# Reordering the head of an eight-core decoder-layer kernel: part of the first query projection ahead of the last adaLN chunk

## What is computed

```
ada = silu(c) @ w_ada + b_ada                 # shift, scale, gate
h = rms_norm(x, norm_g) * (1 + scale) + shift
z = h @ w_in                                  # 8704 columns: q, k, v of three groups, gates, branch B, merges
q = rope(rms_norm(z_q)); k = rope(rms_norm(z_k))     # per group and head
attn = softmax-weighted sum of three dilated causal window attentions
y_a = attn * silu(gate_a); y_b = u * spatial(layer_norm(v_b)) * silu(gate_b)
out = x + gate * ((sig(m_a) * (y_a @ w_branch_a) + sig(m_b) * (y_b @ w_branch_b)) @ w_out)
```

## Time and profile before

| | |
|---|---|
| median of 6 runs | 753.49 us (753.33 to 754.24) |
| the profiled execution's own time | 754.04 us |
| its span on the slowest core (core 7) | 752.5 us |
| spans of the eight cores | 748.7 to 752.5 us |
| PE busy on core 7 | 714.4 us, 95% of the span |
| DVE, ACT, POOL busy | 63%, 48%, 38% |
| DMA, mean over the span | 93 GB/s |

### The profile page before, as it was taken

One profiled execution on the slowest core, in us unless ns is written; L12 is line 12 of the kernel. 1 busy time (PEld: TensorE's weight loads), 2 busy tenths in 40 slices (PEclk: granted clock), 3 DMA queues, 4 the chain that ended last, 5 costly groups with the idle time before them and its releaser, 6 DMA issues.

```text
span 752.5 us, 14671 instructions; the slowest of 8 cores (748.7 to 752.5 us)
## 1 busy us (share of the span) xinstructions
PE 714.4 (95%) x4702; PEld 359.3 (48%) x4702; DVE 471.7 (63%) x788; ACT 361.1 (48%) x687; POOL 289.3 (38%) x370
## 2 busy tenths in 40 slices
PE   7778999999999999999999999999999999999994
PEld 2444455556655554445554444444444444444442
DVE  6437799986587778888788864466664233222333
ACT  3636888878645554556676645565221111111110
POOL 1405243342444455433434002577232343343343
PEclk9879999999999999999999999999999999999998
DMA  8994125034456657531111607139980223111324
GB/s 240 322 181 132 55 85 127 3 51 78 59 84 81 93 75 76 85 58 29 29 29 30 113 1 112 29 49 177 187 233 28 84 86 108 61 56 57 113 58 167
DMA packets 61243, 70.00 MB, mean 93 GB/s; under 512 B 39792, under 2 KB 46064, under 8 KB 60528
## 3 DMA queue, kind: packets, MB, share of 16 engines
q0 software_dynamic: 16352, 22.29, 21.0%
q1 hardware_dynamic: 42368, 38.39, 20.6%
q10 hardware_dynamic: 2448, 8.39, 2.8%
HBM read 74.82 MB, written 8.39 MB: 111 GB/s over the span
## 4 chain that ended last, share of the span: by engine, by line
PE 65%; DVE 9%; DMA 7%; issue 6%; ACT 6%; SPq 3%; POOL 2%; DVEq 0%; ACTq 0%; POOLq 0%
PE ps L249 57%; DVE arena L258 9%; ACT arena L258 6%; DMA arena<-w_ada 3%; SPq L261 3%; PE ps L651 2%; DMA arena<-arena 2%; DMA arena<-w_in 2%; POOL arena L258 2%; PE ps L544 2%; PE ps L687 2%; PE ps L692 1%; PE ps L609 1%; SPq L600 0%; PE ps L1048 0%
## 5 line engine op out<-in xcount | busy, mean ns | idle before, releaser
L249 PE MATMUL ps<-arena 128*128 128x512 bf16 x2596 | 582.5, 380 | 10.0 <-DVE arena L258 7.1
L249 PEld LDWEIGHTS ps<-arena 128*128 128x128 bf16 x2596 | 269.0, 107 | 291.9 <-issue 31.1
L258 POOL TENSOR_TENSOR arena<-arena 128x128 bf16<-128x128 f32 (+5 forms) x308 | 255.5, 838 | 395.3 <-DVE arena L258 332.1
L258 ACT ACTIVATE arena<-ps 128x1024 bf16<-128x1024 f32 (+2 forms) x283 | 192.1, 709 | 263.0 <-PE ps L249 137.1
L258 DVE TENSOR_TENSOR arena<-ps,arena 128x512 bf16<-128x512 f32 (+2 forms) x214 | 166.2, 798 | 58.8 <-PE ps L249 24.4
L258 ACT ACTIVATE arena<-arena 128x8 f32<-128x8 f32 (+7 forms) x264 | 108.9, 423 | 73.3 <-DVE arena L258 49.1
L258 DVE SCALAR_TENSOR_TENSOR arena<-arena,ps 128x512 f32<-128x512 f32 x80 | 54.3, 686 | 110.1 <-PE ps L249 92.1
L258 DVE TENSOR_TENSOR arena<-arena 128x1024 bf16<-128x1024 bf16 (+5 forms) x111 | 78.0, 705 | 23.1 <-POOL arena L258 10.7
L258 DVE TENSOR_REDUCE arena<-arena 128x8 f32<-128x512 bf16 x96 | 65.4, 685 | 42.7 <-ACT arena L258 42.2
L258 DVE SCALAR_TENSOR_TENSOR arena<-arena 128x512 f32<-128x512 f32 (+3 forms) x40 | 33.3, 831 | 11.8 <-DMA arena<-w_ada 4.3
L258 DVE TENSOR_SCALAR arena<-arena 128x512 bf16<-128x512 bf16 (+5 forms) x57 | 27.6, 484 | 11.4 <-DMA arena<-w_ada 7.6
(11 more groups left out here) (42 smaller groups left out, 186.7 us busy)
## 6 DMA issues: line engine op xcount, KB each, us to landing
arena<-x SPq DMA_DIRECT2D x32, 512.0 KB, 5.3
arena<-w_in POOLq DMA_DIRECT2D x9, 1024.0 KB, 14.2
arena<-w_in POOLq DMA_DIRECT2D x32, 256.0 KB, 5.6
arena<-w_ada SPq DMA_DIRECT2D x15, 512.0 KB, 15.0
out<-arena ACTq DMA_DIRECT2D x15, 512.0 KB, 5.6
arena<-w_adag SPq DMA_DIRECT2D x8, 512.0 KB, 7.8
arena<-w_out POOLq DMA_DIRECT2D x2, 1024.0 KB, 23.8
arena<-w_ba POOLq DMA_DIRECT2D x1, 1024.0 KB, 12.9
```

The costliest lines, as they stand in the source:

```text
L249: ins = e.matmul(out_ap, l, r, start=(i == 0), stop=(i == n - 1))
L258: P.op(eng, lambda e: getattr(e, meth)(*a, **kw), reads=reads, writes=writes)
```

## The change

Loads: x tile 3 is loaded ahead of adaLN chunk 2 instead of behind it. The first three q quarters are gated on the landing of x tile 2, the fourth on the second piece of chunk 3 (`wada3_2`), and the k and v quarters follow it in POOL's list. x tile 4 is gated on the fourth q quarter instead of the third.

Order: the tiles 1, 2 and 3 are normalised and transposed ahead of adaLN chunk 2, their scaling moves from ACT to DVE. `phase(0, 0)` and `phase(0, 1)` of the tiles 0, 1 and 2 come ahead of `ada_mm(2)`, their `phase(0, 2)` ahead of `ada_mm(3)`; tile 3 does its three quarters after `ada_ab(3)`. The spins are 8, then 12, then 16 behind the landing of `wada3_4`, instead of 8 and 14.

```diff
-            for t in ((0,), (1, 2), (3,), ())[c]:
+            for t in ((0,), (1, 2, 3), (), ())[c]:
                 x_load(t)
...
         sq_own(1)
-        x_prep(1)
+        rs_own(1)
         spin(4, 7)
         ada_mm(1)
-        ada_sum(2, 0, 3)
         ada_ab(1)
+        sc_own(1)
         x_transp(1, 4)
-        sq_own(2)
-        x_prep(2)
-        x_transp(2, 5)
-        for kc in range(4):
-            x_mods(kc, "act", 0, 2)
-        ada_sum(2, 3, 8)
+        for t in (2, 3):
+            sq_own(t)
+            rs_own(t)
+            sc_own(t)
+            x_transp(t, 3 + t)
+        for t in (0, 2):
+            for kc in range(4):
+                x_mods(kc, "act", t, 2)
+        for p_ in range(3):
+            load_w(0, 0, p_, p_ + 1, ["xs2"])
+        load_w(0, 0, 3, 4, ["wada3_2"])
+        for j in (1, 2):
+            for p_ in range(4):
+                load_w(j, 512 * j, p_, p_ + 1)
+        for t in range(4):
+            x_load(t + 4, gate=[("ws0p3", "ws1p2", "ws2p1", "ws2p3")[t]])
+        ada_sum(2)
         spin(8, 7)
-        ada_mm(2)
-        sq_own(3)
-        x_prep(3)
-        x_transp(3, 6)
-        ada_sum(3, 0, 4)
-        ada_ab(2)
...
-        for j in (0, 1, 2):
-            for p_ in range(4):
-                load_w(j, 512 * j, p_, p_ + 1, ["wada2_6"])
-        for t in range(4):
-            x_load(t + 4, gate=[("ws0p2", "ws1p2", "ws2p1", "ws2p3")[t]])
-        ada_sum(3, 4, 8)
-        spin(14, 7)
-        ada_col(3)
-        for kc in (6, 7):
-            x_mods(kc, "act", 0, 2)
-            x_mods(kc, "dve", 2, 2)
...
+        phase(0, 0, range(3))
+        phase(0, 1, range(3))
+        ada_mm(2)
+        ada_ab(2)
+        for t in (0, 2):
+            for kc in (4, 5):
+                x_mods(kc, "act", t, 2)
+        ada_sum(3)
+        phase(0, 2, range(3))
+        spin(12, 2)
+        spin(16, 2, ["wada3_4"])
+        ada_mm(3)
+        ada_ab(3)
+        for kc in (6, 7):
+            x_mods(kc, "act", 0, 2)
+            x_mods(kc, "dve", 2, 2)
         for j in range(3):
-            phase(0, j)
+            phase(0, j, (3,))
         last(0)
```

More of the change, by code:

```diff
@@ L472, in build_nc @@
         sq_own(1)
-        x_prep(1)
+        rs_own(1)
         spin(4, 7)
         ada_mm(1)
-        ada_sum(2, 0, 3)
         ada_ab(1)
+        sc_own(1)
         x_transp(1, 4)
-        sq_own(2)
-        x_prep(2)
-        x_transp(2, 5)
-        for kc in range(4):
-            x_mods(kc, "act", 0, 2)
-        ada_sum(2, 3, 8)
-        spin(8, 7)
-        ada_mm(2)
-        sq_own(3)
-        x_prep(3)
-        x_transp(3, 6)
-        ada_sum(3, 0, 4)
-        ada_ab(2)
-        for kc in (4, 5):
-            x_mods(kc, "act", 0, 2)
-        for kc in range(6):
-            x_mods(kc, "act", 2, 2)
-        for j in (0, 1, 2):
-            for p_ in range(4):
-                load_w(j, 512 * j, p_, p_ + 1, ["wada2_6"])
-        for t in range(4):
-            x_load(t + 4, gate=[("ws0p2", "ws1p2", "ws2p1", "ws2p3")[t]])
-        ada_sum(3, 4, 8)
-        spin(14, 7)
-        ada_col(3)
-        for kc in (6, 7):
-            x_mods(kc, "act", 0, 2)
-            x_mods(kc, "dve", 2, 2)
+        for t in (2, 3):
[15 more added lines that the diff above has]
+        ada_sum(2)
+        spin(8, 7)
         X("dve", "tensor_copy", ["misc"], ["gcol"], out=gcol, in_=gqk)
```

## The result

The changed kernel takes 759.11 us (median; 757.58 to 761.41) where the kernel before, run beside it, took 753.38 (752.68 to 755.13): a ratio of 1.0074, with a 95% interval of 1.0065 to 1.0082. It is slower by 5.6 us (0.0074 x 753.38); 753.7 with a range to 756.5 was forecast. The profiled execution took 759.17 us at a span of 757.6, on core 4.

What follows compares the result with a forecast made beforehand. TensorE was taken to bound the body (PE 95% busy), leaving only the head to gain. Tile 4's -0.8 plus the clock's +1.0 gave +0.2 us on 753.49: 753.7 us, range 751.0 to 756.5.

Steps and rivals of the forecast that it cites:

- The adaLN chunk: Last adaLN weight load: `wada3_2` at 41.9, whole chunk landing at about 45 us, as before (44.5).
- The fourth q quarter: Weight load gated on `wada3_2`: issued 0.6 us after it, 4.8 us long, landing at 47.3, at latest 50.8.
- the quiet window: Lightly loaded DMA stretch in the earlier profile: 4.8 us for a weight quarter, against 8.3 under load.
- its late bound: Latest landing allowed for x tile 4: 60.5 us, from a quarter at 50.8 plus 9.7.
- the term of x tile 4, the -0.8 us: ACT's start on tile 4, gated on the fourth q quarter: about 57.0 instead of 57.79, 0.8 us gained.
- The gain of 0.8 us from an earlier x tile 4: Same tile 4 claim: ACT starts about 57.0 instead of 57.79, whatever PE has saved.
- PE's own way: PE's path to the first q result of `last(0)`: about 53 (52 to 56) instead of 55.2, gaining 2 us.
- The clock: TensorE's granted clock behind PE's wait before tile 4's transpose: 1.0 us lost, bounds nothing to 2.9.
- the slow rival: PE's wait before tile 4's transpose lowers the clock: 2.9 us, 756.4 with tile 4 at its old time; chance 0.33.
- the case of x tile 4 at its late bound together with the low clock: Tile 4 landing at 60.5 and reduced TensorE clock behind its transpose; left outside the range, no total given.

Runs made afterwards that it cites:

- e3: Changed kernel with x tile 4 not gated at all: 755.96 us, ratio 1.0007 to the kernel before.
- e6: Changed kernel, x tile 4 ungated, chunk 2's columns before q, two chunk 3 sums before `ada_ab(2)`, 16 spins of 28: 753.45 us, ratio 0.9974.
- e1: Changed kernel with x tile 4 gated on the third q quarter again instead of the fourth: 756.44 us, ratio 1.0009 to the kernel before.
- e4: Kernel before with only x tile 4's gate moved, from the third q quarter to the second k quarter: 764.46 us, ratio 1.0097.
- e2: Changed kernel with 40 unused matmuls added on PE ahead of x tile 4's transpose: 759.78 us, ratio 1.006 to the kernel before.
- e8: Kernel before with x tile 4 not gated, nothing else changed: 755.56 us, ratio 0.9995.
- e5: Changed kernel with x tile 4 ungated and the 28 spins ahead of the last adaLN columns left out: 757.30 us, ratio 1.0023.

## Why the prediction was wrong

**The adaLN chunk: right.** `wada3_2` was forecast at 41.9 and landed at 40.0 to 43.0 on the eight cores; the chunk was forecast at about 45 and landed at 43.3 to 45.5.

**The fourth q quarter: the first term mis-sized.** The prediction took the quiet window's 4.8 us, to 47.3, and the loaded 8.3 as its bound. On the latest core of the changed kernel, 4, and on an early one, 1, the DMA views have these issues (queue, count, size, us from issue to landing):

```profile
arena<-w_in POOLq DMA_DIRECT2D x1, 256.0 KB, 6.8
arena<-x SPq DMA_DIRECT2D x1, 512.0 KB, 10.4
...
arena<-w_in POOLq DMA_DIRECT2D x1, 256.0 KB, 4.1
```

It took 6.8 us on core 4, 4.0 to 7.1 on the eight, and landed at 45.5 to 50.3. 50.8 had been the bound, and core 4 came about half a microsecond short of it. Part of the spread is a later start: on cores 1, 2, 5 and 6 the first of its packets move 1.2 us behind the issue, on cores 0, 3, 4 and 7 2.3 to 2.5 us behind it.

**x tile 4: its late bound, on the cores that count.** The chain is the one that the prediction drew, but its term was too small on the late cores. It took 10.4 us on core 4, where 9.7 was taken, and landed at 60.9, with 57.0 forecast and 60.5 as the bound. The 3.9 us between are 1.1 of the gate (42.97 for 41.9), 2.0 of the quarter (6.8 for 4.8), 0.7 of the tile and 0.1 of issue. On core 7, from which every term was taken, the forecast held in this execution: quarter at 47.7, tile at 57.0, first q result at 53.4, transpose at 60.03 where "within 1 us of 60.96" was written. **The step that failed is the term of x tile 4, the -0.8 us: it was made for core 7**, the slowest before, and its late bound was left to the edge of the range. On the core that ended last it measured +2.9 at the transpose. The time is that of the slowest of eight cores. With landings of the same transfer spread from 54.1 to 60.9, the latest one decides, and that lay at the bound.

**The gain of 0.8 us from an earlier x tile 4** did not come: on core 4, ACT began on it at 60.96 and not at about 57.0. Core 7's earlier transpose, 60.03 for 60.96, agrees with the forecast's 0.8 us, but it is not the core that ends last.

**PE's own way: right in the middle, worth nothing at the end.** 52 to 56 was forecast for the first q result, and it came at 51.3 to 55.5. But before, it was 52.0 to 55.2: the latest cores gained nothing, where 2 us had been expected. What was not seen is that `ada_sum(3)` stands behind `ada_ab(2)` on DVE, and that one behind PE's matmuls of quarter 1. DVE's timeline of core 4:

```profile
44.64 0.16 DVE L258 TENSOR_TENSOR arena<-ps,arena 128x4 f32<-128x4 f32 x1 [5.55 <-PE ps L408]
...
45.60 5.88 DVE L258 SCALAR_TENSOR_TENSOR arena<-arena 128x512 f32<-128x512 f32 x7
```

The prediction priced two sums of chunk 2 at 0.75 each and none of chunk 3's behind the wait. By e3 against e6 (ratios 1.0007 and 0.9974) undoing this order, together with 12 spins fewer, is worth 2.5 us.

**The clock: the slow rival's mechanism, at nearly its price.** The rival named the place (the transpose of x tile 4), the point ("x tile 4 after 57.5") and 2.9 us; it had a chance of 0.33. It happened where the prediction said, and cost 2.2 us of the span, against the 1.0 taken for the sum. The forecast's -0.8 + 1.0 became 2.9 + 2.2. The Trainium skill (TensorE: Matmul & The Clock Gate, Part 1, The HAM clock gate) has the throttled clock as the default state that activity releases; the trace agrees in direction, as 0.18 us of work in 2.8 was followed by 0.50, and 1.11 or 1.94 us of waiting was not.

**What was left out of the range.** The rival kept tile 4 "at its old time" and so came to 756.4; the case of x tile 4 at its late bound together with the low clock was left out by name. They are not independent: the same late tile moves the transpose and makes the wait that lowers the clock. By the prediction's own terms that case gives 753.49 + 2.7 (60.5 for 57.79) + 2.9 = 759.1, and by the measured ones 753.49 + 2.9 + 2.2 = 758.6; the changed kernel took 759.11. That the first agrees to the digit is luck, since its two terms are off by 0.2 and 0.7 us in opposite directions.

**Shown and open.** That x tile 4's gate is the cause is shown from both sides: e1 and e3 take it away and the loss goes, e4 adds it alone to the kernel before and a loss comes. That the clock has a part is shown by the cores of one execution (14.2 against 16.5 us to the next transpose) and by core 4 of e2, where the filled wait left it at 1.00. e8 shows that the gain of e6 is not the tile's; how much of that gain is the order of the sums and how much the fewer spins is open. Open, too, is why POOL's queue began 1.2 us after the issue on four cores and 2.3 to 2.5 us after it on the others.

## What to carry to other kernels

A new gate makes a chain of transfers: add their late landings, not their typical ones, and do so for the slowest core, since it sets the time. A late input in front of a dense TensorE stretch is paid twice, by the delay and by the clock behind it, so the two go into one case. Before moving work on one engine, look in the other engines' lists for what stands behind a wait on it: here, sums on DVE stood behind columns on PE, and undoing that, with fewer spins, brought 2.5 us. A wait is priced best up to the next fixed point of the same core: the rest of a span has waits of its own, here one of 2.86 us for a weight load (e4).

## Not expected of the hardware

- One fall of the granted clock cost 2.3 us on each of four cores (16.5 us from this transpose to the next for 14.2), following waits of 3.38 to 7.19 us; a wait twice as long did not cost more behind it. In e4 a wait of 2.60 was followed by it too. In e2 the same wait some 11 us later, of 2.08 or 2.09 us, was followed by 0.50 on core 7 and not on cores 0, 2, 3 and 5.
- Unused matmuls in the place of a wait held the clock (e2, core 4: 1.00 behind the transpose and 14.2 us to the next), and leaving out 28 of them was followed by 0.50 until 57 (e5, core 7).
- The same 256 KB load, issued onto DMA engines that were 8% busy until its first packets (core 4, 43.5 to 45.8) or 31% (core 1, 41.5 to 42.7), took 4.0 to 7.1 us on the eight cores of one execution, and x tile 4 behind it 10.4 us with eight quarters outstanding on the other queue, where such a tile took 3.8 in a quiet window.
